# Attention's entry products of a two-block model in float32: three fp32r passes by row halves, four low halves and the rotation tables on GpSimd

## The reference

```
u  = rmsnorm(h, kv_norm)                  # 256 x 1024
kv = (u @ kv_w).reshape(B, S, 6, 4, 64)   # 1024 x 1536: k_c v_c | k_s v_s | k_w v_w
k_s, k_w = rope(rmsnorm(k_s, ..)), rope(rmsnorm(k_w, ..))
k_cmp = rope(rmsnorm(compress(k_c, ..)))  # gelu(blocks @ w1 + b1) @ w2 + b2
v_cmp = compress(v_c, ..)
u = rmsnorm(h, norm_g)                    # the same h, another gain
z = u @ w_in                              # 1024 x 1072: 1024 query columns, 48 gate columns
q = rope(rmsnorm(z[..., :1024]))
gates = sigmoid(z[..., 1024:] + gate_b)
```

## Time and profile before

| | |
|---|---|
| median of three runs | 2331.18 us (2330.7 to 2337.31) |
| the profiled execution | 2330.57 us, span of its records 2327.5 us |
| PE busy | 2290.6 us, 98% of the span |
| DVE, ACT, POOL busy | 1694.1, 1377.5, 104.5 us |
| granted TensorE clock | 0.997 over the span |
| PE's entry products, from `kv` 0 to the first score | 293.89 to 393.60 us |

### The profile page before, as it was taken

The page is one execution under the profiler, slowest core; times in us unless marked ns, Lnnn a source line. Parts: engine busy times, 40 slices in busy tenths (PEclk is TensorE's granted clock), DMA queues, the critical chain, the costliest instruction groups (busy, mean ns, idle before and its releaser), DMA issues.

```text
span 2327.5 us, 30292 instructions
## 1 busy us (share of the span) xinstructions
PE 2290.6 (98%) x11602; PEld 1900.4 (82%) x11602; DVE 1694.1 (73%) x1615; ACT 1377.5 (59%) x1247; POOL 104.5 (4%) x111
## 2 busy tenths in 40 slices
PE   7999999999999999999999999999999999999998
PEld 7988857988888878888987788888888888888886
DVE  6655555755557776645767779888888888888897
ACT  4633313653356855433567567777777777777775
POOL 0000020000001200000011000000000000000020
PEclk9999999999999999999999999999999999999999
DMA  7555444165625347445343489999999999999992
GB/s 241 182 198 216 145 140 177 68 231 203 216 83 181 109 145 253 175 164 202 118 156 122 147 356 415 416 390 371 382 376 388 367 392 367 391 368 389 369 383 120
DMA packets 205667, 588.53 MB, mean 253 GB/s; under 512 B 9180, under 2 KB 19616, under 8 KB 205584
## 3 DMA queue, kind: packets, MB, share of 16 engines
q1 hardware_dynamic: 198736, 564.28, 64.9%
q0 software_dynamic: 6656, 23.04, 2.6%
q10 hardware_dynamic: 192, 0.05, 0.0%
HBM read 573.19 MB, written 14.16 MB: 252 GB/s over the span
## 4 chain that ended last, share of the span: by engine, by line
PE 96%; DVE 2%; ACT 1%; DMA 1%; issue 0%; DVEq 0%; ACTq 0%
PE ps L1457 9%; PE ps L1456 9%; PE ps L1458 9%; PE ps L805 8%; PE ps L807 8%; PE ps L806 8%; PE ps L1496 4%; PE ps L1495 4%; PE ps L1497 4%; PE ps L683 3%; PE ps L1233 2%; PE ps L1235 2%; PE ps L1234 2%; PE ps L675 2%; PE ps L1167 1%; PE ps L693 1%
## 5 line engine op out<-in xcount | busy, mean ns | idle before, releaser
L2133 DVE TENSOR_TENSOR more_low<-more_parts,high_parts 128x2048 fp32r<-128x2048 f32 x192 | 431.8, 2286 | 33.7 <-ACT high_parts L1563 32.6
L1563 ACT ACTIVATE high_parts<-more_parts 128x2048 fp32r<-128x2048 f32 x192 | 364.4, 1918 | 101.4 <-PE ps L1497 51.8
L1456 PE MATMUL ps<-high_parts,xmh 128*128 128x512 f32 x896 | 352.5, 393 | 0.0
L1458 PE MATMUL ps<-high_parts,xml 128*128 128x512 f32 x896 | 349.1, 390 | 0.0
L2133 DVE TENSOR_TENSOR raw_low<-raw,high_parts 128x2048 fp32r<-128x2048 f32 x144 | 323.8, 2285 | 26.4 <-ACT high_parts L1563 26.4
L1563 ACT ACTIVATE high_parts<-raw 128x2048 fp32r<-128x2048 f32 x144 | 275.9, 1921 | 92.0 <-PE ps L1458 47.6
L1707 ACT ACTIVATE wh<-raw 128x4096 fp32r<-128x4096 f32 (+1 forms) x57 | 196.8, 3452 | 189.8 <-PE ps L807 176.8
L2310 DVE TENSOR_TENSOR wl<-raw,wh 128x4096 fp32r<-128x4096 f32 (+1 forms) x57 | 239.2, 4197 | 71.8 <-ACT wh L1707 71.8
L805 PE MATMUL ps<-wh,xh 128*128 128x512 f32 (+1 forms) x632 | 244.0, 386 | 3.1 <-issue 2.5
L807 PE MATMUL ps<-wh,xl 128*128 128x512 f32 (+1 forms) x632 | 239.7, 379 | 0.0
L806 PE MATMUL ps<-wl,xh 128*128 128x512 f32 (+1 forms) x632 | 239.5, 379 | 0.0
(11 more groups left out here) (551 smaller groups left out, 4303.5 us busy)
## 6 DMA issues: line engine op xcount, KB each, us to landing
more_parts<-in_moe_w_gate SPq DMA_DIRECT2D x78, 1024.0 KB, 5.6
more_parts<-in_moe_w_up SPq DMA_DIRECT2D x66, 1024.0 KB, 7.1
raw<-in_moe_w_down SPq DMA_DIRECT2D x64, 1024.0 KB, 6.6
more_parts<-in_moe_w_down SPq DMA_DIRECT2D x48, 1024.0 KB, 5.9
raw<-in_moe_w_up SPq DMA_DIRECT2D x46, 1024.0 KB, 5.3
raw<-in_w_in SPq DMA_DIRECT2D x22, 2048.0 KB, 8.0
raw<-in_f_w_in SPq DMA_DIRECT2D x20, 2048.0 KB, 8.7
raw<-in_moe_w_gate SPq DMA_DIRECT2D x34, 1024.0 KB, 6.7
```

Of the source, the lines that this page charges most:

```text
L1456: mm(o, xmh[:, k, :], hi[:, cs], start=(k == 0), stop=False)
L1458: t = mm(o, xml[:, k, :], hi[:, cs], start=False, stop=(k == KD - 1))
L1563: fn(part_high(j), part_raw(j), ACT.Copy).then_inc(hi_done, 1)
L2133: v.tensor_tensor(part_low(j), part_raw(j), part_high(j).bitcast(F32), ALU.subtract).then_inc(lo_done, 1)
```

## The change

All the entry's products become split products. ACT makes the high parts of both normalised streams (`uh`, `ubh`) and DVE the low parts (`ul`, `ubl`) from the same PSUM banks, which `e` and `f` now hold two each. `entry_product` multiplies a weight tile in two row halves, each for both token tiles. ACT makes the ten high halves, in three buffers used in turn (`wmh` 0 and 1 and a new one, `high_x`), each after the products that read the buffer before. DVE makes the six low halves of `kv` 0, `b_in` 0 and `b_in` 1, POOL the four of `kv` 1 and `kv` 2. The gate columns leave the plan of the slots: POOL loads them at the program's start into a buffer of their own, with a high and a low part. The 14 rotation tables move from DVE to POOL. Each of the two `cmp` tiles gets a bank and a release of its own. The last window product moves ahead of the last turned keys, and `scores(0)` now waits until ACT has emptied the whole ring `a`. On DVE the third query rotation moves behind the positions, the fourth behind the gates. The lines of the changed kernel are about 30 to 140 higher.

```diff
-    for t in range(3):
+    for t in range(2):
         tile("b_in", t)
...
+        ENTRY_HIGH = {("kv", 0): (0, 1), ("b_in", 0): (0, 1), ("b_in", 1): (2, 0), ("kv", 1): (1, 2), ("kv", 2): (0, 1)}
+        ENTRY_AFTER = {("b_in", 0, 0): ("kv", 0, 0), ("b_in", 0, 1): ("kv", 0, 1), ("b_in", 1, 1): ("b_in", 0, 0),
+                       ("kv", 1, 0): ("b_in", 0, 1), ("kv", 1, 1): ("b_in", 1, 0), ("kv", 2, 0): ("b_in", 1, 1),
+                       ("kv", 2, 1): ("kv", 1, 0)}
...
+            def entry_product(key, hi_, lo_, low_at=None, tokens=None, between=None):
+                banks = []
+                for half in range(2):
+                    me.see(mh_ready)
+                    if low_at is None:
+                        me.see(ml_ready)
+                    else:
+                        pe.wait_ge(low_made, low_at + half)
+                    hi, lo = entry_high(key, half), entry_view(key, half, raw_low)
+                    for m, ring in enumerate((me.v, me.a)):
...
+                        for kk_ in range(4):
+                            k = 4 * half + kk_
+                            mm(o, hi_[:, k, ms], hi[:, kk_, :], start=(k == 0), stop=False)
+                            mm(o, hi_[:, k, ms], lo[:, kk_, :], start=False, stop=False)
+                            t = mm(o, lo_[:, k, ms], hi[:, kk_, :], start=False, stop=(k == KD - 1))
...
+                        if between and half and m == 0:
+                            between()
...
-            turned(0)
-            keys_values(0)
-            turned(1)
-            product(me.a, ("kv", 0), 1, uT)
...
+            entry_product(("kv", 0), uh, ul, tokens=(1, 2))
+            entry_product(("b_in", 0), ubh, ubl, tokens=(3, 4))
+            entry_product(("b_in", 1), ubh, ubl)
...
+            entry_product(("kv", 1), uh, ul, low_at=1, between=hidden_products)
...
             turn_keys(0)
-            window_part(me.v, 0, 256)
+            window_part(me.a, 1, 1)
+            released(("kv", 2), me.a)
             turn_keys(1)
-            window_part(me.a, 1, 256)
...
             pe.wait_ge(causal_ready, 2)
-            pe.wait_ge(a_read, me.a.n - 1)
+            drained(me.a)
             scores(0)
...
+            high_entry(("kv", 0), 0)
+            high_entry(("kv", 0), 1)
+            high_tile(0, uh, "kv_norm")
+            squares(0)
+            high_tile(1, uh, "kv_norm")
+            squares(1)
+            high_tile(0, ubh, "b_norm")
+            square_root()
+            high_entry(("b_in", 0), 0)
+            high_tile(1, ubh, "b_norm")
...
+            ffn(0, beside=lambda: low_tile_of(0, uh, ul, "kv_norm"), ahead=lambda: low_entry(("kv", 0), 0))
+            low_tile_of(1, uh, ul, "kv_norm")
+            low_entry(("kv", 0), 1)
+            me.see(norm_sq, M)
+            v.tensor_scalar(small[:, 2:4], small[:, 0:2], 1.0 / D, EPS, ALU.mult, ALU.add).then_inc(norm_ms, 1)
+            low_tile_of(0, ubh, ubl, "b_norm")
+            roots()
+            low_entry(("b_in", 0), 0)
...
+            po.dma_start(gates_raw[:], A["b_w_in"][0].rearrange("(k p) n -> p k n", p=P)[:, :, 1024:1024 + 3 * NH]).then_inc(small_in, 16)
...
+            for key in (("kv", 1), ("kv", 2)):
+                for half in range(2):
+                    po.wait_ge(mh_ready, entry_high_at[(*key, half)])
+                    nc.gpsimd.tensor_tensor(entry_view(key, half, raw_low), entry_view(key, half),
+                                            entry_high(key, half).bitcast(F32), ALU.subtract).then_inc(low_made, 1)
```

More of the change, by code:

```diff
@@ L980, in _ @@
             compressed_in = me.v.n
-            arrived(pe, ("b_in", 2))
+            me.see(mh_ready)
+            me.see(ml_ready)
             for m in range(M):
-                product(me.v, ("b_in", 2), m, ubT, w=3 * NH)
-            released(("b_in", 2), me.v)
+                b, ms = me.v.claim(pe), slice(m * P, (m + 1) * P)
+                for k in range(KD):
+                    o = ps[:, b, 0:3 * NH]
+                    mm(o, ubh[:, k, ms], gates_high[:, k, :], start=(k == 0), stop=False)
+                    mm(o, ubh[:, k, ms], gates_low[:, k, :], start=False, stop=False)
+                    t = mm(o, ubl[:, k, ms], gates_high[:, k, :], start=False, stop=(k == KD - 1))
+                t.then_inc(v_filled, 1)
             pe.wait_ge(v_read, compressed_in)
-            b = me.a.claim(pe)
             for kv in range(2):
@@ L1768, in _, with high_entry, high_tile @@
             ffn(0)
+            def high_entry(key, half):
+                arrived(act, key)
+                if (*key, half) in ENTRY_AFTER:
+                    act.wait_ge(*entry_used[ENTRY_AFTER[(*key, half)]])
+                elif key == ("kv", 0):
+                    act.wait_ge(u_done, FFN_END["ffn0"])
+                fn(entry_high(key, half), entry_view(key, half), ACT.Copy).then_inc(mh_ready, 1)
+            entry_banks = {}
+            def high_tile(m, dst, gain):
+                for j, ring in enumerate((me.e, me.f)):
+                    if (m, j) not in entry_banks:
+                        entry_banks[m, j] = ring.take(act)
+                    b = entry_banks[m, j]
+                    for i in range(4):
+                        k, ts = 4 * j + i, slice(m * P, (m + 1) * P)
+                        t = fn(dst[:, k, ts], ps[:, b, i * P:(i + 1) * P], ACT.Copy, scale=col(gain, k))
+                    t.then_inc(norm_h, 1)
+            high_entry(("kv", 0), 0)
[8 more added lines that the diff above has]
+            high_tile(1, ubh, "b_norm")
             fn(ident_r[:], C("ident"), ACT.Copy).then_inc(causal_ready, 1)
             fn(causal_r[:], C("neg_causal"), ACT.Copy).then_inc(causal_ready, 1)
-            for m in range(M):
-                b = me.f.take(act)
-                for i in range(4):
-                    k, ts = 4 + i, slice(m * P, (m + 1) * P)
-                    fn(uT[:, k, ts], ps[:, b, i * P:(i + 1) * P], ACT.Copy, scale=col("kv_norm", k))
-                    t = fn(ubT[:, k, ts], ps[:, b, i * P:(i + 1) * P], ACT.Copy, scale=col("b_norm", k))
-                t.then_inc(f_read, 1)
-                squares(m)
-            square_root()
             def root(n, rows=P):
@@ L1806, in _ @@
             marks["kvc_a"] = me.a.n
-            root(NH // 2)
+            high_entry(("b_in", 0), 1)
+            high_entry(("b_in", 1), 0)
+            high_entry(("b_in", 1), 1)
+            act.wait_ge(small_in, GATES_IN)
+            fn(gates_high[:], gates_raw[:], ACT.Copy).then_inc(mh_ready, 1)
             queries(0)
@@ L1812, in _ @@
             root(NH // 2)
+            root(NH // 2)
             me.see(gate_ready)
             fn(gate[:], gate[:], ACT.Sigmoid).then_inc(gated, 1)
-            b = me.a.take(act)
-            fn(hidden_n, ps[0:NG * NCMP, b, :], ACT.Copy).then_inc(a_read, 1)
+            high_entry(("kv", 1), 0)
+            high_entry(("kv", 1), 1)
+            for kv in range(2):
+                b = me.a.take(act)
+                fn(hidden_n[:, kv * CH:(kv + 1) * CH], ps[0:NG * NCMP, b, 0:CH], ACT.Copy).then_inc(a_read, 1)
             for m in range(M):
@@ L1834, in _ @@
             keys_values(1)
-            root(NG)
             root(NG)
@@ L1840, in _ @@
             root(NG)
+            root(NG)
             turned_keys(0)
+            b = me.a.take(act)
+            fn(vv[:, 1, 1, :, 0:HD], ps[:, b, 0:256].rearrange("p (g d) -> p g d", g=NG), ACT.Copy,
+               scale=small[:, 7:8]).then_inc(a_read, 1)
             turned_keys(1)
@@ L1844, in _ @@
             fn(cs[:], cs[:], ACT.Exp, scale=SCALE).then_inc(cexp_ready, 1)
-            b = me.a.take(act)
-            fn(vv[:, 1, 1, :, 0:HD], ps[:, b, 0:256].rearrange("p (g d) -> p g d", g=NG), ACT.Copy,
-               scale=small[:, 7:8]).then_inc(a_read, 1)
             def probs(i):
```

215 lines of the change are left out of this document (132 added, 83 removed).

## The result

The changed kernel takes **2336.5 us** (median of eleven executions) against 2331.18 before: 1.0023 times as long, 95% interval 1.0015 to 1.003. The forecast was 2326.0 with a range of 2321 to 2332, so the time lies outside the range and on the slower side, though by less than the 0.3% that counted as no change. Two more executions, the profiled one among them, ran at a low granted clock (0.557 and 0.716 over the span; 3835 and 3213 us) and are left out here (with them the median is 2337.35), so the readings are from a second profile of the same, unedited kernel (`again`).

What follows compares the result with a forecast made beforehand. PE's rate was taken to bound the entry of attention: of 12.5 us saved, 1.1 go at the start and 6.25 behind the keys, leaving 5.15, so 2331.18 becomes 2326.0 us. The range was 2321 to 2332.

Steps and rivals of the forecast that it cites:

- PE's own time: Entry of attention: split products save PE 12.5 us, after 1.6 us more for the gates' narrow matmuls.
- the start and the second weight: Entry, kv 0 to b_in 0: PE waits 1.0 us for the second weight's halves; kv 0's early halves cost nothing.
- every product at the full-clock rate: Entry's split matmuls: steps of 0.227, 0.118 and 0.112 us for 512, 256 and 128 columns.
- the transfers: Trip through DRAM: released 2 us earlier, issues end near 320, PE reads at 327.7.
- The keys: Before scores(0): POOL's kv 2 low halves, 4.1 us each, hold DVE's first key step 3.85 us; 6.25 us lost.
- The start: Program's start: the gates' own 192 KB load runs beside the first weights, costed at nothing (up to 0.5 us).
- DVE is not held: Rival, keys: DVE's chain starts at 360.45, undelayed by POOL; 8.95 us saved, 2322.2; chance 0.23.
- POOL much slower: Rival, POOL's halves: no gain at 6.6 us per half, 2337.7 at 8.25; chance 0.12.
- little left, 2329: Rival, entry: narrow gates, first matmuls after waits and the 1.0 us twice as dear; 2 us remain; chance 0.08.

Runs made afterwards that it cites:

- fill_behind: Changed kernel with SP's two compressed-matrix loads held back and POOL's fill of the zeroed tile behind its two low halves of kv 1; 2331.41 us.
- zero_late: Changed kernel with POOL's fill of the zeroed tile moved behind the issues of the trip through DRAM; 2339.93 us.
- gates_between: Changed kernel with the gates' 48 narrow matmuls spread, six behind every three wide ones, in the second half of b_in 1; 2333.89 us.
- fills_wait: `zero_late` with SP's loads of the two compressed matrices held back until the DRAM write and the loads back are done; 2338.95 us.
- three: Changed kernel with the fill behind the DRAM trip, SP's two loads held back and the gates among wide matmuls; 2331.25 us.
- five: `three` with all four late low halves on DVE instead of POOL, and ACT's high halves of kv 1 ahead of the sigmoid; 2329.57 us.
- six: `five` with the last window product of kv 2 put ahead of the compressed scores; 2328.3 us.
- gates_load_late: Changed kernel with the load of the gates' weights moved from the program's start to behind ffn0; 2339.76 us.
- seven: `six` with POOL's fill of the zeroed tile waiting for DVE's second low half of kv 1; 2327.86 us.

## Why the prediction was wrong

**PE's own time: right.** Split products step by 0.229 to 0.233 us at full clock (0.227), narrow matmuls by 0.111 (0.112), and `fill_behind` shows the first three pieces within 0.6 us of the arithmetic.

**The first step that failed: "the start and the second weight", 1.0 us.** Measured 3.6. DVE's queue was written out there with the mean squares at no price, and POOL's fill was costed at nothing, its cover measured against the trip through DRAM alone. The question put to each POOL instruction was what waits for it, and not which DVE instruction it stands beside. Holds were priced for the subtractions with two operands only. The Trainium skill (SBUF — State Buffer, Who interferes with whom) has the rest of the rule: tensor_scalar can run in a mode that takes both port pairs, and then whoever has them keeps the other waiting for the whole instruction, while an instruction with two SBUF inputs contends only with a GpSimd one that reads. The rows here agree on both (4.68 beside the fill; 2.29 undisturbed beside it), and the row of 0.68 us in the trace of before had shown it. In one point they do not agree: that section of the Trainium skill gives the ports to whoever issues first, and the small step's record begins 1.05 us before the fill's. Nor was the hold between two-operand steps, which the prediction priced in the keys, applied to the tables (2.96 and 2.36 us above).

**The second: every product at the full-clock rate.** The trace of before has no fall of the clock in the entry, where PE never stands; the prediction took the rate over, with no term for a fall of the clock. After 3.6 us of standing PE ran at 1.2 GHz to 317, and the two `b_in` products took 3.1 us more than predicted; `zero_late`, without that wait, has no such fall there. Then the clock fell in the gates, with 2.8 us more there and 2.2 in the compressed products. `gates_between` keeps the wait of 3.6 us, spreads the narrow matmuls and has no fall there; `fill_behind` keeps them in a row, has only 0.9 us of that wait, holds SP's loads back as well, and is at half clock for 3.4 us instead of 10.2. So neither the narrow matmuls in a row nor the earlier wait is shown to be the cause by itself. What decides when the clock falls stays open.

**The third, hidden by the first: the transfers.** The prediction moved the trip through DRAM 2 us earlier and kept its duration. With a tile out of the ring, SP's 2 MB loads come sooner and meet it. As the changed kernel runs, this costs PE nothing, because PE is late; `zero_late` shows 4.6 us of it when PE is not.

**The keys: mechanism right, size a little off.** POOL's half costs 4.5 us, not 4.1; the Trainium skill (GPSIMD Engine Reference, Elementwise — side-by-side cycle accounting) gives 4497 ns, and the rows (4.50 to 4.62 where DVE does not disturb it) agree. DVE's first step was held 4.34 us (3.85), and the piece took 38.5 (37.1). Where `kv` 1 comes sooner, as in `fill_behind`, the pair holds DVE 6.6 us.

**The start.** `again` reaches `kv` 0 2.5 us later than before. 1.8 us of it lies in the first products after 16 us, which in some executions step at half the rate although 1.00 is granted there: 5 and 6 matmuls in the two stretches of 2 us from 16 us on, where before has 10 and 11. They do so in `again`, `fills_wait`, `three`, `five` and `six`, and not in the other seven. Not explained; the load, which the prediction priced at up to 0.5 us, is neither shown to cost it nor excluded.

**The rivals.** "DVE is not held" and "POOL much slower" are excluded by the rows above. The case "little left, 2329" came closest: it named the wait of 1.0 us and the narrow gates, at twice their price each, but they came at 3.6 us and, by the clock, 2.8 us over, for reasons that it did not have. No case had a time beyond 2332 with POOL at its usual price. The missing rivals were a hold of DVE by POOL anywhere but in the keys, and a fall of the clock.

## What to carry to other kernels

When work is moved to GpSimd, lay each of its instructions, fills too, beside what VectorE does in that stretch, the smallest statistic included: a step of two numbers can stand for a whole fill, and what is queued behind it pays. When a kernel's fp32 products are replaced by cheaper passes, give each new wait on TensorE, and each row of narrow matmuls, a second price, that of a stretch at half clock, and put wide products where PE would stand. And when a tile leaves a ring of buffers, all later loads move; look at what they now run beside.

## What was not expected of the hardware

- A GpSimd fill of 128x4216 (3.61 to 3.65 us), which reads nothing, held a tensor_scalar of VectorE of 128x2 or 128x8, with its operands in SBUF, to its own end in eight of the twelve profiles behind the result (4.68 to 4.95 us instead of 0.17 to 0.28). It let a 128x2048 subtraction of two SBUF operands pass (2.29 us, `gates_load_late`), and in the kernel before tensor_scalars of 128x128 that read PSUM (0.34 us each, 294.1 to 295.3). In the eight the small step's record begins 1.0 to 1.3 us before the fill's, and yet it ended with the fill; why the later of two records wins stays open.
- The granted clock fell to 0.50 within waits of 3.6 to 4.6 us on TensorE, and not at one of 0.9 in the same place; it also fell with no wait just before it: in `again` in a row of 48-column matmuls, in `six` and `seven` in one of 30 columns.
